# Three transformer blocks in float32: the products turned round, activations stationary and split weights streaming as 512 columns

## The reference

```python
# first layer
mod = silu(c) @ w_ada + b_ada;  shift, scale, gate = split(mod, 3)
h = rms_norm(x) * (1 + scale) + shift
q_sb, k_sb, v_sb, z_sb, q_r, k_r, v_r, z_r = split(h @ w_in)   # 8 heads of 128 each
oa = stick_breaking_attention(norm(q_sb), norm(k_sb), v_sb) * silu(z_sb)
ob = head_group_norm(retention(rotary(q_r), rotary(k_r), v_r)) * silu(z_r)
x = x + gate * (concat(oa, ob) @ w_out)
# second layer: short convolution, state space (SSD), memory attention; then @ w_out0
# third layer: latent attention (w_uq, w_ukv, 16 heads), memory attention; then @ w_out1
out = rms_norm(x)
```

## Time and profile before

| | |
|---|---|
| three timed runs | 1932.32, 1932.55, 1935.68 us, median 1932.55 |
| span of the profiled execution, first to last instruction | 1933.9 us |
| PE busy, PEld busy | 1829.7 us (95%), 1776.6 us (92%) |
| DVE busy, ACT busy | 1168.0 us (60%), 912.6 us (47%) |
| read from HBM | 346.87 MB, 180 GB/s over the span |

### The profile page before, as it was taken

The page is one execution under the profiler, slowest core; times in us unless marked ns, Lnnn a source line. Parts: engine busy times, 40 slices in busy tenths (PEclk is TensorE's granted clock), DMA queues, the critical chain, the costliest instruction groups (busy, mean ns, idle before and its releaser), DMA issues. The chain is left out here.

```text
span 1933.9 us, 35014 instructions
## 1 busy us (share of the span) xinstructions
PE 1829.7 (95%) x14439; PEld 1776.6 (92%) x14439; DVE 1168.0 (60%) x1437; ACT 912.6 (47%) x1116; POOL 80.4 (4%) x95
## 2 busy tenths in 40 slices
PE   2698999999999989999999999999989999999997
PEld 2688999999998989999999999999989999888997
DVE  3987767554466645667556665764464546566744
ACT  2333444454356444666444556643345454455642
POOL 0111000000010000000000000000000000000000
PEclk9898999999999999999999999999999999999999
DMA  8897888445454553665645455555546564443453
GB/s 288 333 346 282 298 285 283 148 138 167 142 143 130 185 165 115 202 184 176 184 134 153 142 156 149 177 193 180 182 138 179 153 198 139 123 114 119 153 180 105
DMA packets 168329, 350.98 MB, mean 181 GB/s; under 512 B 10032, under 2 KB 26544, under 8 KB 162048
## 3 DMA queue, kind: packets, MB, share of 16 engines
q1 hardware_dynamic: 161168, 298.34, 50.2%
q0 software_dynamic: 7024, 50.66, 7.0%
HBM read 346.87 MB, written 2.10 MB: 180 GB/s over the span
## 5 line engine op out<-in xcount | busy, mean ns | idle before, releaser
L391 PE MATMUL psG<-hA,w_hi 128*128 128x256 f32 x3904 | 1133.9, 290 | 57.0 <-DVE w_lo L322 36.8
L393 PE MATMUL psG<-hA,w_lo 128*128 128x256 f32 x3904 | 1112.3, 285 | 0.0
L392 PE MATMUL psG<-lA,w_hi 128*128 128x256 f32 x3904 | 1112.3, 285 | 0.0
L322 DVE TENSOR_TENSOR w_lo<-raw,w_hi 128x1024 fp32r<-128x1024 f32 (+1 forms) x568 | 689.5, 1218 | 629.8 <-ACT w_hi L316 628.4
L316 ACT ACTIVATE w_hi<-raw 128x1024 fp32r<-128x1024 f32 (+1 forms) x568 | 584.0, 1035 | 595.1 <-PE psG L393 505.8
L391 PEld LDWEIGHTS psG<-hA,w_hi 128*128 128x128 f32 x3904 | 755.7, 194 | 74.7 <-issue 58.1
L392 PEld LDWEIGHTS psG<-lA,w_hi 128*128 128x128 f32 x3904 | 756.2, 194 | 3.5 <-issue 2.9
L393 PEld LDWEIGHTS psG<-hA,w_lo 128*128 128x128 f32 x3904 | 755.5, 194 | 0.0
L1049 DVE SCALAR_TENSOR_TENSOR ada_sum<-ada_ring,silc,ada_sum 128x2048 f32<-128x2048 f32 x48 | 112.5, 2346 | 3.6 <-DMA ada_ring<-in_w_ada 3.6
L413 ACT ACTIVATE P<-psG 128x1024 f32<-128x1024 f32 (+2 forms) x60 | 59.7, 996 | 104.9 <-PE psG L393 104.9
L391 PE MATMUL psG<-kvH,w_hi 128*128 128x256 f32 x192 | 56.9, 297 | 0.9 <-ACT P L413 0.9
(11 more groups left out here) (294 smaller groups left out, 1485.1 us busy)
## 6 DMA issues: line engine op xcount, KB each, us to landing
raw<-in_w_in SPq DMA_DIRECT2D x352, 512.0 KB, 3.8
raw<-in_w_out SPq DMA_DIRECT2D x128, 512.0 KB, 3.9
ada_ring<-in_w_ada POOLq DMA_DIRECT2D x48, 1024.0 KB, 7.3
raw<-in_mem_w SPq DMA_DIRECT2D x32, 512.0 KB, 8.7
raw<-in_w_uq SPq DMA_DIRECT2D x24, 384.0 KB, 3.5
raw<-in_w_ukv SPq DMA_DIRECT2D x16, 512.0 KB, 4.1
raw<-in_w_in SPq DMA_DIRECT2D x8, 384.0 KB, 3.3
P<-in_memT SPq DMA_DIRECT2D x1, 2048.0 KB, 25.9
```

The costliest lines, as they stand in the source:

```text
L322: nc.vector.tensor_tensor(w_lo[:, s, :, 0:cols], raw[:, s, :, 0:cols], w_hi[:, s, :, 0:cols], ALU.subtract).then_inc(lo_ready, 1)
L391: nc.tensor.matmul(out, hi, x_hi, start=k == 0 and f % 2 == 0, stop=False)
L392: nc.tensor.matmul(out, hi, x_lo, start=False, stop=False)
L393: last = nc.tensor.matmul(out, lo, x_hi, start=False, stop=end)
```

## The change

**Operands change places.** The stationary operand is now a half of the activation tile (128 features x 128 tokens), and the weights stream as 512 columns. A chunk has 12 matmuls of 512 columns instead of 24 of 256. Products of 384 columns (C2, UQ) have 12 of 384 instead of 18 of 256; DT, 128 columns wide, stays as it was.

**The result is turned back.** It now has tokens on its partitions, in two banks for the two halves of the tokens. ACT copies it into a new buffer `tok` (L411), PE turns it by 8 transposes of 128x128 (6 or 4 for narrower blocks) into the same banks after the first chunk of the next block (`turn_product`, L422), and then ACT places it in `P` or DVE adds it to the residual. 71 blocks are turned, with 518 transposes. The products that end a layer turn their last block at once, before the norm. Blocks of values aren't turned: ACT copies them with tokens on the partitions, and the 80 transposes of values and DVE's copies of them fall away, in the UKV products for a half of each block.

**Slots.** `w_lo` takes the place of `raw` in memory, so a raw slot is free only when PE has used the chunk, and the ring has five slots instead of four.

**Loops are written out**, all counts are constants, and some waits for whole products (`landed`) become waits for the blocks that are needed, or stand later. A few hooks move by one or two positions.

```diff
-SLOTS = 4
+SLOTS = 5
...
         raw = sb("raw", [NP, SLOTS, 2, 512])
+        w_lo = sb("w_lo", [NP, SLOTS, 2, 512], F32R, place=top[0] - SLOTS * 4096)
         w_hi = sb("w_hi", [NP, SLOTS, 2, 512], F32R)
-        w_lo = sb("w_lo", [NP, SLOTS, 2, 512], F32R)
...
         def load_weights(sp, g):
-            with turns(sp, g.bodies) as i:
-                for bb in range(g.body):
-                    for c in range(g.chunks):
-                        n = g.c0 + bb * g.chunks + c
-                        per = g.body * g.chunks
-                        src = g.src(i * g.body + bb, c)
-                        sp.wait_ge(lo_ready, i * per + (n + 1))
-                        sp.dma_start(raw[:, n % SLOTS, :, 0:g.cols], src)\
-                          .then_inc(raw_loaded[n % SLOTS], 16)
-
-        def split_hi(act, n, i, per, cols):
-            act.wait_ge(raw_loaded[n % SLOTS], i * (per // SLOTS * 16) + 16 * (n // SLOTS + 1))
-            act.wait_ge(chunk_used, i * per + (n + 1))
-            nc.scalar.activation(w_hi[:, n % SLOTS, :, 0:cols], raw[:, n % SLOTS, :, 0:cols], ACT.Copy)\
-              .then_inc(hi_ready, 1)
-
-        def split_lo(dve, n, i, per, cols):
-            dve.wait_ge(hi_ready, i * per + (n + 1))
-            s = n % SLOTS
+            for b in range(g.blocks):
+                for c in range(g.chunks):
+                    n = g.c0 + b * g.chunks + c
+                    if n >= SLOTS:
+                        sp.wait_ge(chunk_used, n + 1 - SLOTS)
+                    sp.dma_start(raw[:, n % SLOTS, :, 0:g.cols], g.src(b, c)).then_inc(raw_loaded[n % SLOTS], 16)
+
+        def split_hi(act, n):
+            s, cols = n % SLOTS, CHUNKS[n][0].cols
+            act.wait_ge(raw_loaded[s], 16 * (n // SLOTS + 1))
+            nc.scalar.activation(w_hi[:, s, :, 0:cols], raw[:, s, :, 0:cols], ACT.Copy).then_inc(hi_ready, 1)
+
+        def split_lo(dve, n):
+            s, cols = n % SLOTS, CHUNKS[n][0].cols
+            dve.wait_ge(hi_ready, n + 1)
             nc.vector.tensor_tensor(w_lo[:, s, :, 0:cols], raw[:, s, :, 0:cols], w_hi[:, s, :, 0:cols],
                                     ALU.subtract).then_inc(lo_ready, 1)
 
-        def split_first(eng, split, g):
-
-            for n in range(AHEAD):
-                split(eng, g.c0 + n, 0, 0, g.cols)
...
+        def run_split(eng, split, g, hook, hook_first, block_done, turn_done):
+
+            for b in range(g.blocks):
+                for c in range(g.chunks):
+                    n = g.c0 + b * g.chunks + c
+                    if c == 1 and n >= 2:
+                        turn_done(*CHUNKS[n - 2])
+                    if hook_first:
+                        hook(b, 2 * c)
+                    if n + AHEAD < len(CHUNKS):
+                        split(eng, n + AHEAD)
+                    if not hook_first:
+                        hook(b, 2 * c)
+                    hook(b, 2 * c + 1)
+                block_done(b)
+
+        def no_hook(b, p):
+            pass
+
+        def take_product(act, g, b):
+
+            products_done(act, g, b + 1)
+            bank, t = set_of(g, b), g.turn_number(b)
+            if g.turned[b] is None:
+                g.place(b, bank).then_inc(evacuated, 1)
+            elif not g.turns(b):
+                g.tokens(b, bank).then_inc(evacuated, 1)
+            else:
+                if t >= 2:
+                    act.wait_ge(turned, t - 1)
+                out, src = tok[:, t % 2, :, 0:g.cols], psG[:, bank:bank + 2, 0:g.cols]
+                if tuple(g.turned[b]) == (0, 2):
+                    g.tokens(b, bank)
+                    out = tok[:, t % 2, :, 0:2 * NP].rearrange("p h (t d) -> p h t d", t=2)
+                    src = psG[:, bank:bank + 2, :].rearrange("p h (t d) -> p h t d", t=4)[:, :, 0::2, :]
+                nc.scalar.activation(out, src, ACT.Copy).then_inc(drained, 1)
+
+        def turn_product(pe, g, b):
+
+            if not g.turns(b):
                 return
-            with turns(eng, g.bodies - peel) as i:
-                turn(i, g.bodies == 1)
-            if peel:
-                turn(g.bodies - 1, True)
-
-        def no_hook(i, bb, p):
-            pass
-
-        def run_products(pe, g, hook=None, lead=None):
-
-            per = g.body * g.chunks
-
-            def turn(i, hook):
-                for bb in range(g.body):
-                    bank = set_of(g, bb)
-                    pe.wait_ge(evacuated, i * g.body + (g.b0 + bb + 1))
-                    for c in range(g.chunks):
-                        n = g.c0 + bb * g.chunks + c
-                        s = n % SLOTS
-                        if g.ready:
-                            pe.wait_ge(*g.ready(c))
-                        pe.wait_ge(lo_ready, i * per + (n + 1 + CREDIT))
-                        for kk in range(2):
-                            k = 2 * c + kk
-                            x_hi, x_lo = g.x(k)
-                            for f in range(g.cols // NP):
-                                hi, lo = (w[:, s, kk, f * NP:f * NP + NP] for w in (w_hi, w_lo))
-                                out = psG[:, bank + f // 2, (f % 2) * S:(f % 2 + 1) * S]
-                                end = k == 2 * g.chunks - 1 and (f % 2 == 1 or f == g.cols // NP - 1)
-                                nc.tensor.matmul(out, hi, x_hi, start=k == 0 and f % 2 == 0, stop=False)
-                                nc.tensor.matmul(out, hi, x_lo, start=False, stop=False)
-                                last = nc.tensor.matmul(out, lo, x_hi, start=False, stop=end)
-                            if kk == 1:
-                                last.then_inc(chunk_used, 1)
-                            if hook:
-                                hook(i, bb, k)
-
-            if lead:
-                assert g.bodies == 2
-                turn(0, lead)
-                turn(1, hook)
-            else:
-                with turns(pe, g.bodies) as i:
-                    turn(i, hook)
-
-        def copy_out(tile0, per_block=4, last=None):
-
-            def evacuate(block, bank):
-                n = per_block
-                out = P[:, at(tile0 + block * n, n), :]
-                src = psG[:, bank:bank + 2, :].rearrange("p b (h s) -> p (b h) s", h=2)[:, 0:n, :]
-                return nc.scalar.activation(out, src, ACT.Copy)
-            return evacuate
-
+            t, bank = g.turn_number(b), set_of(g, b)
+            pe.wait_ge(drained, t + 1)
+            for i in range(len(g.turned[b])):
+                for h in range(2):
...
+        def run_products(pe, g, hook=no_hook):
+
+            for b in range(g.blocks):
+                bank = set_of(g, b)
+                if g.b0 + b >= SETS:
+                    pe.wait_ge(evacuated, g.b0 + b + 1 - SETS)
+                for c in range(g.chunks):
+                    n = g.c0 + b * g.chunks + c
+                    s = n % SLOTS
+                    if g.ready:
+                        pe.wait_ge(*g.ready(c))
+                    pe.wait_ge(lo_ready, n + 1)
+                    for kk in range(2):
+                        k = 2 * c + kk
+                        first, end = k == 0, k == 2 * g.chunks - 1
+                        hi, lo = w_hi[:, s, kk, 0:g.cols], w_lo[:, s, kk, 0:g.cols]
+                        x_hi, x_lo = g.x(k)
+                        if g.turned[b] is None:
+                            out = psG[:, bank, 0:S]
+                            nc.tensor.matmul(out, hi, x_hi, start=first, stop=False)
+                            nc.tensor.matmul(out, hi, x_lo, start=False, stop=False)
+                            last = nc.tensor.matmul(out, lo, x_hi, start=False, stop=end)
+                        else:
+                            for h in range(2):
+                                out, half = psG[:, bank + h, 0:g.cols], slice(h * NP, h * NP + NP)
+                                nc.tensor.matmul(out, x_hi[:, half], hi, start=first, stop=False)
+                                nc.tensor.matmul(out, x_hi[:, half], lo, start=False, stop=False)
+                                last = nc.tensor.matmul(out, x_lo[:, half], hi, start=False, stop=end)
+                        if kk == 1:
+                            last.then_inc(chunk_used, 1)
+                        hook(b, k)
+                    if c == 0 and n and not (b == 0 and CHUNKS[n - 1][0].residual):
+                        turn_product(pe, *CHUNKS[n - 1])
+            if g.residual:
+                turn_product(pe, g, g.blocks - 1)
 
 
         GATE = {"f1": 0, "yb": 4, "sc": 8, "f2": 10, "zc": 11}
 
```

More of the change, by code:

```diff
@@ L83, with __init__, turns, turn_number @@
 class Gemm:
-    def __init__(self, kt, blocks, src, x, cols=512, ready=None):
+    def __init__(self, kt, blocks, src, x, place=None, cols=512, ready=None, turned=lambda block: range(4),
+                 tokens=None):
         self.chunks, self.blocks, self.src, self.x, self.cols, self.ready = kt // 2, blocks, src, x, cols, ready
[L90 to L95, removed]
```

(35 more changed lines are left out.)

639 lines of the change are left out of this document (304 added, 335 removed).

## The result

| | before | with the change |
|---|---|---|
| median of 5 runs each, us | 1932.55 (1930.8 to 1935.68) | 1942.01 (1938.38 to 1950.32) |
| ratio | | 1.0049, interval 1.0032 to 1.0066 |
| span of the profiled execution, its own time, us | 1933.9, 1935.68 | 1939.8, 1941.63 |
| mean granted clock of TensorE | 0.982 | 0.976 |
| forecast, us | | 1836 (1816 to 1882) |

A forecast was written before the change was run, and what follows sets the result against it. It took PE's product rhythm as the bound, except DVE and landings in MEM: span 1933.9 - 142.8 - 6.5 + 45.6 + 6.3 - 8 + 6 + 3 = 1837.5 us, median 1836, range 1816 to 1882.

The forecast's parts named there:

- What sets 120 ns: PE's products: the weight load outlasts a 256-column stream by 13 ns; at 512 columns the stream wins, 216 ns.
- rival 1: PE's products: the 13 ns stay at every width, 227 ns a product, +68 us, 1904; chance 0.08.
- Rival 4: PE's products: the load isn't hidden beside a 512-column stream, 330 ns a product, 2558 us; chance 0.03.
- The mis-sized term: Products outside MEM: 5,952 of 512 columns save 24 ns each, -142.8 us; 384-column chunks (C2, UQ) save 6.5 us.
- Part 2: Turns on PE's path: 422 more at 108 ns each, +45.6 us, waits for ACT's copy covered.
- rival 3: Turns on PE: 275 ns each in place of 108, +70 us, 1906; chance 0.03.
- The cover: Block ends: turns 2.6 us later hide ACT's 1.02 us copy; without it up to 1 us a block.
- rival 2: Feeding and hand-offs bind: SBQK and SBV lose all, turned blocks 0.2 to 0.5 us each; 1858 to 1880, chance 0.17.
- Part 3: Ends of OUT, OUT0 and OUT1: copy, eight turns and hand-offs before the residual adds, +6.3 us.
- Part 4: PE's six waits for L413, mostly at stage starts: removed except one ahead of OUT1, -8 us.
- Part 5: Weight feeding: raw slots held until PE's use, tighter in SBQK and SBV, +6 us; new waits +3 us.
- the sign of a miss: PE's waits on `w_lo` after 333 us growing beyond 10 us would make the prediction fall.

The follow-up runs named there:

- bench: Standalone run, 48 products of each form in a row, nothing else computed; at 512 columns fp32r takes 227 ns, bfloat16 216 ns.
- after_4: The changed kernel with four ring slots instead of five; 2121.99 us, 1.0982 of the time before the change.
- bf16_after: The changed kernel with all operands of products in bfloat16, result less exact; 1882.53 us, 0.9714 of the time before the change.
- no_turn: The changed kernel without tok, turns and second copies, blocks copied or added straight from PSUM (wrong values); 1865.5 us, 0.9636 of the time before the change.
- no_turn_hooks: The changed kernel without tok, turns and second copies, and with the hooks of OUT and OUT1 at their positions of before; 1857.91 us, 0.9616 of before.

## Why the prediction was wrong

**The step that failed is "What sets 120 ns".** It held the 13 ns of a product to be a weight load longer than the stream, which a stream of 512 columns would cover. They are a fixed addition of an fp32r product at full clock: 227 ns, as rival 1 had it, to which I gave 0.08. Rival 4 (330 ns) is out by the same rows. Three readings misled. The earlier trace rows are at the lowered clock, where the addition doesn't appear; it doesn't appear at 512 columns there either, so they said nothing on full clock. The earlier trace rows are products of another type, float32, and bench shows that type at 214 to 216 ns, without the 13 ns. That the load starts with the product before holds at 227 ns too (1000.44, above) and proves no bound. And no row of before had an fp32r product of another width at full clock, the only thing that tells a constant from a load; the range should have reached to 1904 for it. The mis-sized term: 5,952 products at 227 save 13.3 ns each, 79 us and not 142.8; those of 384 columns, 173.3 ns (160 + 13.3; bench has 174), save 2.6 us and not 6.5. Together +68 us.

**Part 2, the turns:** 0.109 us each as in the earlier trace rows, right; rival 3 (275 ns) is out. The cover for their hand-offs failed. It was argued from ScalarE's 47% and the 2.6 us between the block's end and the turn. But ScalarE works in order, and its second copy makes it stand until TensorE has turned; everything behind it, logs, splits and through them VectorE's sums, comes later. This is rival 2's mechanism, and the average of 0.4 us a block lies in its 0.2 to 0.5, though it falls on few blocks. Turns and ends of layers cost 76.5 instead of 51.9: +25 us (+28 by the ratios).

**Part 3, ends of layers:** 6.3 predicted. In OUT1 the last product starts at 1920.50, the copy at 1920.92, the turns at 1922.00, the adds at 1923.13: 2.2 us from the last product's end, against about 2.1 forecast. From the last product's end to the end of the span it is 3.6 us more than before; what is left, 1.4, is the sum of squares behind the adds, which ran at the lowered clock (L1634, 3.44 us for eight records; before L1612, 1.99).

**Part 4, waits removed:** 8 forecast, about 3 gained. Only the wait ahead of OUT1 was seen to be one for the low part that stays; those ahead of OUT and OUT0, 2.45 us each, are of the same kind. The profile put all three down to the copy L413, which ended at nearly the same time. +5 us.

**Part 5, feeding:** right for `w_lo` (from 333 us on TensorE waits 6.3 us for it, 5.7 before, where 10 was the sign of a miss), but the slack was thin, as after_4 shows. In SBQK and SBV nothing was gained, as rival 2 had it: from the first product of SBQK to the first of RTQK it is 143.7 us (184.67 to 328.32), before 143.0 (189.77 to 332.80). The moved hooks were put, with other new waits, at 3 us and cost 4 to 8 us in OUT and OUT1. By the clock, 0.982 to 0.976, some 23 us more are run at 1.2 GHz (2 x 0.024 x 1939.8 less 2 x 0.018 x 1933.9), part of them behind the new short waits (two stretches behind L1721); how this divides among the terms stays open.

**The sum's frame:** the median was taken 1.3 us under the span. The profiled execution's own time lies 1.8 us over it: +3 us.

1836 + 68 + 25 + 8 + 5 + 3 = 1945, measured 1942. That it comes so close is partly luck: the medians of the groups differ by up to 3 us, the hooks' term may be half as large, and the forecast's 9 us for feeding and new waits were never measured by themselves. The products' term is shown by bench and bf16_after, the turns' by no_turn, the hooks' less surely, by no_turn_hooks. Each rival had been priced as if the others were false; rivals 1 and 2 came true together, which gives 1836 + 68 + 22 to 44, and that sum stood nowhere.

## What to carry to other kernels

A time per instruction that is split into a constant and a share of the width needs two widths of the same type at the same clock; without them both splits belong into the range. A copy that one engine's program takes in order and that waits for another engine's answer holds up everything queued behind it, even at a busy share of 50%; what that costs depends on what stands there, little in most blocks here and some 3 us a block in SBZ and RTZ. The profile's name for a wait is a guess where two things end close together: before a wait is counted as removed, look which of them stays. Where results are wanted in the streaming layout anyway, as the values here, the turned form pays by itself; where they must be turned back, the turn took about as much here as the wider stream gave, and the moved hooks and the waits did the rest.

## What the runs showed of the hardware

- An fp32r product costs its stream plus 13 ns at full clock at 256, 384 and 512 columns, and its bare stream at the lowered clock. Bfloat16 in its place takes 216 ns at 512 columns.
- The distance doesn't depend on whether the stationary operand changes, nor, within some 3 ns, on its size (bench: 227 ns with 64 rows, 230 with 64 columns).
- Waits of 2 us on TensorE can be dearer than they look. Behind the one that ends at 536.83, of 2.21 us, L1721 took 1.22 us in place of 0.59, and the lowered clock lasted until about 540.3; behind the one of 2.20 us that ends at 569.80 products stood at the lowered clock from 571.3 to 574.4. Behind a third, of 2.21 us at 602.74, the clock stayed.

```profile
539.41 0.77 PE L451 MATMUL psG<-w_hi,hA 128*128 128x512 f32 x1
539.98 0.53 PE L452 MATMUL psG<-w_lo,hA 128*128 128x512 f32 x1
540.35 0.39 PE L453 MATMUL psG<-w_hi,lA 128*128 128x512 f32 x1
```
